# Sixteen indirect stores of token rows on GpSimd, without their waits for TensorE

## The reference

```
logits = xt @ w_router                      # 256 tokens, 8 experts
top_logit, top_idx = top_k(logits, 2)       # each token goes to two experts
gates = softmax(top_logit)
for each expert e, over the tokens that chose it:
    hid = silu(x @ w_gate[e]) * (x @ w_up[e])      # 1024 -> 3584
    y  += gate * (hid @ w_down[e])                 # 3584 -> 1024
```

## Time and profile before

| | us |
|---|---|
| median of three runs | 1319.14 |
| the profiled execution, its device time | 1318.12 |
| the profiled execution, span from first to last instruction | 1316.3 |
| TensorE (PE) busy | 1286.2 (98% of the span) |
| VectorE (DVE) busy | 673.3 (51%) |
| ScalarE (ACT) busy | 251.9 (19%) |
| GpSimd (POOL) busy | 59.9 (5%) |
| mean granted TensorE clock | 0.993 of full speed |

### The profile page before, as it was taken

How to read it: one execution, slowest core, us unless ns; L and a number is a source line. 1 busy time by engine, 2 the same in 40 slices (tenths; PEclk the granted TensorE clock), 3 DMA queues, 4 the chain that set the end, 5 groups by cost and what they waited for, 6 DMA issues and landing times.

```text
span 1316.3 us, 36736 instructions
## 1 busy us (share of the span) xinstructions
PE 1286.2 (98%) x16198; PEld 849.3 (65%) x16198; DVE 673.3 (51%) x943; ACT 251.9 (19%) x386; POOL 59.9 (5%) x50
## 2 busy tenths in 40 slices
PE   9999999999899999999999999999999999999988
PEld 9998899988767444544666773554556655354444
DVE  5885555554875666155155335516605705433461
ACT  5564544443753100000000000000000000000000
POOL 1001000000000330000000000000000000000042
PEclk9999999999999799999999999999999999999999
DMA  9867555565424699999999999999999999999994
GB/s 322 264 212 229 189 185 176 187 224 192 184 97 179 269 403 419 415 420 418 415 419 419 417 419 417 418 417 417 419 417 419 406 416 418 399 418 417 419 407 159
DMA packets 114209, 442.68 MB, mean 336 GB/s; under 512 B 9284, under 2 KB 55700, under 8 KB 83348
## 3 DMA queue, kind: packets, MB, share of 16 engines
q1 hardware_dynamic: 107904, 424.75, 81.8%
q10 hardware_dynamic: 4820, 11.53, 2.5%
q0 software_dynamic: 1344, 4.20, 0.8%
HBM read 434.12 MB, written 12.08 MB: 339 GB/s over the span
## 4 chain that ended last, share of the span: by engine, by line
PE 71%; SPq 11%; DMA 9%; DVE 4%; issue 2%; ACT 2%; ACTq 0%; DVEq 0%
PE bank L2089 16%; PE bank L2040 15%; PE bank L2058 9%; PE bank L1590 8%; PE bank L1592 7%; PE bank L1591 7%; SPq L531 6%; PE bank L2070 5%; SPq L534 4%; DMA more_ring<-in_moe_w_up 4%; DMA raw<-in_moe_w_down 2%; DMA raw<-in_moe_w_up 2%; DMA hidT<-in_moe_w_gate 1%; ACT w_hi L697 1%; DVE w_lo L991 1%
## 5 line engine op out<-in xcount | busy, mean ns | idle before, releaser
L991 DVE TENSOR_TENSOR w_lo<-raw,w_hi 128x2048 fp32r<-128x2048 f32 x62 | 141.4, 2289 | 98.0 <-ACT w_hi L697 98.0
L2089 PE MATMUL bank<-more_ring,hidT 128*32 128x256 f32 x3072 | 172.1, 379 | 0.7 <-DMA more_ring<-in_moe_w_down 0.7
L2040 PE MATMUL bank<-more_ring,xT 128*32 128x512 f32 (+1 forms) x1632 | 164.2, 549 | 0.0
L1509 DVE TENSOR_TENSOR sums<-raw 128x768 f32<-128x768 f32 (+1 forms) x32 | 35.0, 1094 | 223.8 <-DMA raw<-in_moe_w_up 118.0
L2089 PEld LDWEIGHTS bank<-more_ring,hidT 128*32 128x32 f32 x3072 | 101.6, 110 | 66.8 <-DMA more_ring<-in_moe_w_down 1.2
L2089 PE MATMUL bank<-raw,hidT 128*32 128x256 f32 x2304 | 127.8, 379 | 2.5 <-DMA raw<-in_moe_w_down 2.5
L1590 PE MATMUL bank<-ht_hi,w_hi 128*128 128x256 f32 x464 | 128.7, 277 | 1.5 <-DVE ht_lo L1005 1.5
L2040 PE MATMUL bank<-raw,xT 128*32 128x384 f32 (+1 forms) x1344 | 130.1, 532 | 0.0
L1591 PE MATMUL bank<-ht_lo,w_hi 128*128 128x256 f32 x464 | 128.3, 276 | 0.0
L1592 PE MATMUL bank<-ht_hi,w_lo 128*128 128x256 f32 x464 | 128.3, 276 | 0.0
L697 ACT ACTIVATE w_hi<-raw 128x2048 fp32r<-128x2048 f32 x62 | 118.7, 1920 | 37.6 <-PE bank L1592 37.6
(11 more groups left out here) (331 smaller groups left out, 1826.6 us busy)
## 6 DMA issues: line engine op xcount, KB each, us to landing
more_ring<-in_moe_w_down SPq DMA_DIRECT2D x64, 1024.0 KB, 21.8
raw<-in_moe_w_down SPq DMA_DIRECT2D x48, 1024.0 KB, 20.9
more_ring<-in_moe_w_gate SPq DMA_DIRECT2D x40, 1024.0 KB, 21.5
more_ring<-in_moe_w_up SPq DMA_DIRECT2D x40, 1024.0 KB, 22.5
raw<-in_moe_w_gate SPq DMA_DIRECT2D x32, 768.0 KB, 21.5
raw<-in_moe_w_up SPq DMA_DIRECT2D x32, 768.0 KB, 21.4
more_ring<-in_moe_w_up SPq DMA_DIRECT2D x32, 768.0 KB, 21.0
raw<-in_moe_w_gate SPq DMA_DIRECT2D x24, 1024.0 KB, 22.6
```

What stands on the lines that cost most here:

```text
L991: nc.vector.tensor_tensor(w_lo[:, slot, :], raw[:, slot_raw, :], plain(w_hi[:, slot, :]), SUB).then_inc(split_ready, 1)
L1509: nc.vector.tensor_tensor(t1, b12, b11, SUB).then_inc(sum_ready, 1)
L2040: ins = nc.tensor.matmul(out_banks[j][GTOK * c:GTOK * c + GTOK, 0:w], xT[:, j, kt, :], chunk[:, c], start=kt == 0, stop=kt == KT - 1)
L2089: ins = nc.tensor.matmul(banks[1 + j // 2][GTOK * c:GTOK * c + GTOK, 256 * (j % 2):256 * (j % 2) + 256], hidT[sup][:, g, m, :], ring_place ...
```

## The change

It takes away the two lines ahead of each store, the wait for `up_used` and the increment of `pool_pace`. Nothing else differs: the waits for `slots_ready` and `rows_zeroed` ahead of the loop stay, and the order of the stores stays.

```
             for t in range(TT):
                 for i in range(2):
                     for c in range(4):
-                        pool.wait_ge(up_used, UP_USED[8 * t + 4 * i + c])
-                        pool.sem_inc(pool_pace, 1)
                         to = bass.IndirectOffsetOnAxis(ap=slot[:, t, i, c:c + 1], axis=0)
                         nc.gpsimd.indirect_dma_start(out=x_rows, out_offset=to, in_=xs[:, t, 256 * c:256 * c + 256],
                                                      in_offset=None).then_inc(spread[t][i], 16)
```

## The result

The changed kernel takes 1328.57 us (median of 6 runs: five from 1324.38 to 1330.46, whose own median is 1327.70, and a disturbed one of 1358.96 at a lower clock that the comparison leaves out); the kernel before, run beside it, 1318.28 us (1314.20 to 1319.28, 6 runs). The ratio is 1.0076, with a 95% interval from 1.0056 to 1.0095. The forecast was 1318.2 with a range from 1315.8 to 1320.5: the changed kernel is 0.8% slower, and outside the range. The profiled execution took 1326.76 us, with a span of 1324.9, 8.6 us more than before's.

The account below looks back on a forecast made before the run. DMA transfers, slightly longer than TensorE's work, were taken to bound the kernel. 0.74 us from two stores moved into the hole plus closer later stores gave 0.9 us gain: median 1318.2 us, range 1315.8 to 1320.5.

Parts of the forecast that it names:

- The bound: Through the experts, DMA transfers need 107.2 us an item against PE's 105.8, so DMA engine time sets the end.
- the hole: DMA engines nearly idle at 450 to 460, share 0.17; two more stores moved there save 0.74 us of the 0.9.
- The upper end of the sum: 1.5 us gained if nothing slows the stores and the first starts at 448.6, nearly nine before 458.5.
- SyncE's wait at line 576: SyncE's 3.1 us wait for the last store before loading `xr`; claimed to vanish wholly, at no gain.
- PE: nothing: Claimed TensorE's time is unchanged: item 1's rows arrive earlier without use, and crowded chunks still land before they are read.
- Rival S: Slower: back-to-back stores hold VectorE's sums at 465.76 to 476.7, PE 3.8 us late, 1322.9 at full price; chance 0.07.
- The rule of the Trainium skill: VectorE in a two-port mode and GpSimd lock shared ports, the second fully blocked; weighed against the change, for the slower rival.
- The test at the end of the prediction: Stores before 450 and an end moved over 2.6 us would mean DMA time doesn't carry item 0's start to the end.

Follow-up runs that it names:

- e17: Changed kernel with four small memsets of parts of `xr` between stores, which come every 1.9 us without waiting for TensorE; 1317.57 us, ratio 0.9997.
- e1: Changed kernel keeping only the wait and increment ahead of the first store; 1317.69 us, ratio 0.9998.
- e6: Changed kernel with four memsets of `xr` (3 us) ahead of the first store, the rest free; 1325.42 us, ratio 1.0058.
- e9: The changed kernel again, unaltered, on another chip; 1327.72 us, ratio 1.0081.
- e12: Changed kernel with 8 tiny matmuls more at the start of TensorE's program; 1328.70 us, ratio 1.0075.
- e4: Changed kernel with 32 tiny matmuls ahead of everything in TensorE's program; 1327.16 us, ratio 1.0079.
- e8: The kernel before, all waits kept, with 32 tiny matmuls ahead of TensorE's program; 1327.01 us, ratio 1.0065.
- e3: Changed kernel with four small memsets of an added tile between stores, no wait for TensorE; 1324.15 us, ratio 1.0047.

## Why the prediction was wrong

- The bound was read rightly, and the rule that follows from it held: time of the DMA engines lost or gained at the start of item 0 comes out at the end. It was applied to 0.9 us in the hole, and came true, within about 1 us, with 8.4 us lost in and behind it.
- The stores' times were right. First at 449.2 forecast and at 448.71 found; seven started by 458.5 and seven found (the eighth at 458.63); about 90 GB/s in 450 to 460 and 93 found. The sixteenth came at 468.78, earlier than 471.5, because VectorE's later sums, which were to slow the last four, were themselves late. The upper end of the sum was met with the first store only, 448.71 for 448.6: three stores took 1.24 to 1.43 us, and seven and not nearly nine were in the hole.
- SyncE's wait at line 576 went away as forecast, at no gain. The `xr` load was to go at 483 and went at 494.49, 11.5 us late, as TensorE was.
- The step that failed is "PE: nothing". It looked at data only: which rows and chunks arrive when. It took for granted that GpSimd's issuing has no effect on an engine that waits for none of it. In its place the runs show 61 weight loads in the 16.3 us from 455.3 to 471.6, item 0 11.3 us longer, and the kernel 0.8% slower. The rows of before could not show the contrary: the first five stores follow each other with a gap of 0.30 us, the others come later, and from the first at 451.95 to the sixteenth at 479.47 it is 1.83 us from one to the next in the mean, against (468.78 - 448.71) / 15 = 1.34 after. The prediction priced the sixteen waits at no busy time, and bounded the change at 0 to 1.5 us of gain, with nothing on the other side. The waits also kept the stores apart, and what that was worth the trace of before doesn't show, so the sum should have had an end on the slower side: five stores in a row were a known state, sixteen an unknown one. Why GpSimd's row of stores slows TensorE stays open.
- Rival S had the sign, 7% and a time of 1322.9, but not the mechanism. VectorE wasn't held. A sum beside the back-to-back stores took 0.96 us, and VectorE sat idle for 19.89 us while TensorE was slow (timeline of VectorE, after):

```profile
456.26 0.96 DVE L1516 TENSOR_TENSOR sums<-sums,raw 128x768 f32<-128x768 f32 x1
477.11 0.96 DVE L1507 TENSOR_TENSOR sums<-raw 128x768 f32<-128x768 f32 x1 [19.89 <-PE bank L2056]
```

- The rule of the Trainium skill, page "SBUF — State Buffer", section "SBUF: two separate sides", that was weighed for S didn't bring the loss: no run here shows VectorE blocked by a store. It speaks of VectorE and GpSimd, and the engine that lost time was TensorE. The prediction told only the half of it that is about two-port modes. The same section gives `tensor_tensor`, which the sums are, no such mode, and has an instruction with two SBUF inputs contend only with one of GpSimd that reads SBUF; whether a store that takes its rows' places from `slot` counts as one it doesn't say. The stores beside sums were again the slower ones, 1.24 and 1.43 us for 0.96 (at 454.08 and 455.63 in after).
- In the same passage the prediction counts seven stores beside the sums from 465.76 to 476.7; the trace of before has six, from 467.51 to 475.97. Nothing else hangs on it.
- The test at the end of the prediction, stores before 450 and an end moved by over 2.6 us, was met, but its conclusion was wrong. It said that the DMA engines' time then doesn't carry the start of item 0 to the end. It does, to within about 1 us.
- Of the gain itself: e17 has the early stores without the slow stretch, and its ratio is 0.9997 (0.9985 to 1.0010). The 0.9 us forecast are 0.0007, inside that interval, so they are neither confirmed nor refuted. The forecast's time, 1318.2, fits e17 (1317.57), not the changed kernel.

## What to carry to other kernels

A wait that looks idle may be keeping instructions apart: before taking it away, ask how densely the instructions behind it have ever been seen to run, and if they haven't, leave room on the slower side. If a row of indirect stores must go early beside TensorE's work, spread it out, by its own small instructions if not by waits (1.9 us apart cost nothing here), and look at the pace of TensorE's weight loads, since the page's busy share hides it: 98% in both kernels. And what holds in one group of runs has to be tried again, on another chip too and with an unchanged kernel beside it: e1 would have passed for a cure.

## What the runs showed of the hardware that was not expected

- Beside unpaced indirect stores TensorE's groups of four weight loads came every 0.70 us instead of 0.32, and later only about 25 loads in 10.6 us, at a granted clock of 1.00 and with the operands there. With 64 bytes a row in place of 1024 it was the same. The pace came back 1.7 to 2.1 us after the last store was made, in all twelve runs that had it.
- The same kernel had this on one chip (item 0 at 116.0 us) and not on another (104.6 us).
- Without added matmuls or tiles, item 0's matmuls began to follow one another at 446.46 to 449.56 us, depending on the run (e6, e9). With eight tiny matmuls at the start of TensorE's program it was 452.27 (e12), with 32 of them 458.72 and 458.47 (e4, e8), and with a tile of 128 bytes a partition more 455.53 (e3). So 32 matmuls cost 9 to 12 us, the tile 6 to 9 and eight matmuls 3 to 6, each but the first from a single execution. What part of the program pays for this was not followed up.
- Item 0 took 104.6 us where the clock was already granted at 1.00 at its start and 1.7 us more where it was 0.50 for the first microseconds. Whether both come in executions of one kernel was not looked at; e1's ten have mean clocks from 0.991 to 0.997 and times from 1312.80 to 1320.02.
